# Panel order in the gates' stage, and where sums, dots and the residual stand in the merge's tail, of a two-block transformer kernel

## The reference

```python
mod_x = (silu(c) @ ada_w + ada_b).reshape(6, D)          # six rows of 1024; rows 2 to 5 are used here
x_z, x_u, x_v, x_gates = ...                             # columns of hx @ w_in
y_gdn = rms_norm(o_x, gdn_norm_g) * silu(x_z)            # o_x from the scan
u = gelu(x_u); v = layer_norm(gelu(x_v))                 # the spatial gating unit
y_sgu = u * (W_s v + b)                                  # a 128x128 mixer over positions, 8 groups
g_a, g_b = split(sigmoid(x_gates))
merged = g_a * (y_gdn @ w_a) + g_b * (y_sgu @ w_b)
x = x + mod_x[2] * (merged @ w_o)
h = rms_norm(x) * (1 + mod_x[4]) + mod_x[3]              # goes to the router and the experts
# and, for the second block, whose turn comes later:
mod_2 = silu(c_2) @ w_ada_2[0] + b_ada_2[0]              # 3 rows for x, and 3 for the context
```

## Time and profile before

| what | value |
|---|---|
| median of 3 runs | 1771.29 us (1769.92 to 1771.68) |
| profiled execution, its own time | 1775.53 us |
| its span | 1773.8 us |
| mean granted TensorE clock | 0.915 |
| PE busy | 1546.5 us (87%) |
| DVE busy | 812.2 us (46%) |
| ACT busy | 371.3 us (21%) |
| gates' stage, first to last start on PE | 468.96 to 611.84 us |
| merge's stage, first to last start on PE | 615.75 to 725.34 us |

### The profile page before, as it was taken

How to read it: one execution, slowest core, us unless ns; L and a number is a source line. 1 busy time by engine, 2 the same in 40 slices (tenths; PEclk the granted TensorE clock), 3 DMA queues, 4 the chain that set the end, 5 groups by cost and what they waited for, 6 DMA issues and landing times. The chain is left out here.

```text
span 1773.8 us, 19527 instructions
## 1 busy us (share of the span) xinstructions
PE 1546.5 (87%) x7573; PEld 901.5 (51%) x7573; DVE 812.2 (46%) x1512; ACT 371.3 (21%) x700; POOL 190.3 (11%) x280
## 2 busy tenths in 40 slices
PE   4999968789999698876789868999889899999977
PEld 2877756578644344442234323444444447656563
DVE  2344548444536558632111123356564315576553
ACT  3222245111111100110000011000450124642230
POOL 0000016500000000001000000000350001212340
PEclk9899989677899799787899988999999899999998
DMA  9331002230577677579999992524311222121120
GB/s 351 98 95 48 1 1 50 84 85 11 183 260 258 235 275 246 226 309 411 408 366 367 388 344 103 190 95 159 103 37 35 95 68 75 48 95 48 49 72 24
DMA packets 132299, 283.62 MB, mean 160 GB/s; under 512 B 28744, under 2 KB 39272, under 8 KB 126955
## 3 DMA queue, kind: packets, MB, share of 16 engines
q1 hardware_dynamic: 128608, 266.65, 42.1%
q0 software_dynamic: 3600, 15.73, 2.2%
HBM read 312.77 MB, written 4.19 MB: 179 GB/s over the span
## 5 line engine op out<-in xcount | busy, mean ns | idle before, releaser
L2707 PE MATMUL ps<-hT,ring 128*128 128x512 f32 x256 | 114.8, 606 | 3.1 <-PEq L2614 2.7
L1395 PE MATMUL ps<-ring,hTx 128*128 128x512 f32 x256 | 112.1, 594 | 1.9 <-PEq L176 1.8
L327 DVE SCALAR_TENSOR_TENSOR ada_acc<-ring,cact,ada_acc 128x512 f32<-128x512 f32 x154 | 104.1, 747 | 0.5
L631 PE MATMUL ps<-hTx,ring 128*128 128x256 f32 x384 | 91.6, 394 | 5.3 <-PEq L176 5.3
L2342 PE MATMUL ps<-hT,ring 128*128 128x512 f32 x208 | 90.4, 592 | 0.0
L631 PEld LDWEIGHTS ps<-hTx,ring 128*128 128x128 f32 x384 | 75.1, 198 | 19.8 <-issue 8.0
L2707 PEld LDWEIGHTS ps<-hT,ring 128*128 128x128 f32 x256 | 48.9, 194 | 62.9 <-issue 62.9
L1395 PEld LDWEIGHTS ps<-ring,hTx 128*128 128x128 f32 x256 | 48.3, 191 | 60.5 <-issue 60.5
L1928 PE MATMUL ps<-ring,hTx 128*32 128x512 f32 x384 | 53.8, 711 | 26.0 <-DMA ring<-in_expert_w 26.0
L722 DVE SCALAR_TENSOR_TENSOR conv<-xpad,taps,conv 128x512 f32<-128x512 f32 (+1 forms) x96 | 63.6, 663 | 3.4
L2342 PEld LDWEIGHTS ps<-hT,ring 128*128 128x128 f32 x208 | 39.5, 190 | 48.5 <-issue 48.3
(11 more groups left out here) (528 smaller groups left out, 2745.8 us busy)
## 6 DMA issues: line engine op xcount, KB each, us to landing
ring<-in_expert_w SPq DMA_DIRECT2D x24, 2048.0 KB, 15.4
far<-in_expert_w SPq DMA_DIRECT2D x24, 2048.0 KB, 18.2
ring<-in_w_in SPq DMA_DIRECT2D x16, 2048.0 KB, 11.6
ring<-in_ada_w SPq DMA_DIRECT2D x12, 2048.0 KB, 9.5
ring<-in_w_ada SPq DMA_DIRECT2D x12, 2048.0 KB, 9.3
ring<-in_w_in_c SPq DMA_DIRECT2D x10, 2048.0 KB, 7.9
ring<-in_expert_w POOLq DMA_DIRECT2D x32, 512.0 KB
far<-in_expert_w POOLq DMA_DIRECT2D x32, 512.0 KB
```

What stands on the lines that cost most here:

```text
L327: ins = dve.scalar_tensor_tensor(out=part, in0=slot[:, kt], scalar=c[:, kt:kt + 1], in1=part, op0=ALU.mult, op1=ALU.add)
L631: ins = pe.matmul(ps[:, j % BANKS, s * L:(s + 1) * L], slot[:, kt, (j % 4) * P:(j % 4 + 1) * P], (hTc, hTx)[s][:, kt], start=(kt == 0), st ...
L1395: ins = pe.matmul(ps[:, 2 + i % BANKS], hTx[:, kt, t * P:(t + 1) * P], stream.slot(n)[:, kt], start=(kt == 0), stop=(kt == KT - 1))
L2707: ins = pe.matmul(bank, slot[:, kt, j % 4 * P:(j % 4 + 1) * P], hT[:, kt], **edge)
```

## The change

It makes three edits in the stream and the gates' stage, and two in the merge's tail.

In the gates' stage the panels' order becomes uvg0, rest0, uvg1, rest1, ... uvg7, rest7, where it was uvg0, uvg1, rest0, uvg2, rest1, ... uvg7, rest6, rest7. `uvg[1]` becomes panel 18, and is issued ahead of panel 17 in the scan's last step (`issue_ahead`). The scan's two borrowed slots swap their roles, so that the one given back early is that of panel 18. `total(k)` stands behind panel k + 1, no longer behind panel k + 2. In the merge's tail each `total` stands behind the whole `w_out` panel, and `dot(5)` and `put(4)` come ahead of both halves of the residual.

```diff
+    def issue_ahead(self, sp, n):
+        sp.wait_ge(self.used[n % RING], n // RING)
+        self.load(sp, n)
+        self.ahead.add(n)            # issue() skips the wait and load of a panel in this set
...
-        for i in range(9):
-            if i < 8:
-                uvg.append(len(stream.panels))
-                add_cols(w_in, COL_Z + (2 + i) * PANEL)
-            if i:
-                rest.append(len(stream.panels))
-                add_cols(ada, (3 + i) * PANEL)
+        for i in range(8):
+            uvg.append(len(stream.panels))
+            add_cols(w_in, COL_Z + (2 + i) * PANEL)
+            rest.append(len(stream.panels))
+            add_cols(ada, (4 + i) * PANEL)
...
-                slot_a, slot_b = (... for i in (2, 1))
+                slot_a, slot_b = (... for i in (1, 2))
...
-                                    stream.issue(sp, uvg[1] + 1)
+                                    stream.issue_ahead(sp, uvg[1])
...     (and gdn_lent[0::2] and [1::2] swap places where PE frees them)
-                                if i // TT >= 2:
-                                    total(pe, i // TT - 2)
+                                if i // TT:
+                                    total(pe, i // TT - 1)
...
-                        total(pe, 6)
                         total(pe, 7)
...     (merge: PE)
-                                if t == 0:
-                                    total(pe, 3 + i)
                             stream.free(pe, n)
+                            total(pe, 3 + i)
...     (merge: DVE)
                         put(dve, 3)
+                        dot(dve, 5)
+                        put(dve, 4)
                         residual(0)
-                        put(dve, 4)
-                        dot(dve, 5)
                         residual(1)
                         put(dve, 5)
```

More of the change, by code:

```diff
@@ L131, in __init__ @@
         self.issued = 0
+        self.ahead = set()
         self.taken = 0
@@ L140, in issue @@
             n = self.issued
-            if n >= RING and self.panels[n](self.slot(n)):
-                sp.wait_ge(self.used[n % RING], n // RING)
-            self.load(sp, n)
+            if n not in self.ahead:
+                if n >= RING and self.panels[n](self.slot(n)):
+                    sp.wait_ge(self.used[n % RING], n // RING)
+                self.load(sp, n)
             self.issued += 1
+    def issue_ahead(self, sp, n):
+        sp.wait_ge(self.used[n % RING], n // RING)
+        self.load(sp, n)
+        self.ahead.add(n)
     def free(self, eng, n):
@@ L788, in build @@
                 xk6 = vdec[:, :, :, :].rearrange("p a u c -> p (a u c)").rearrange("p (u c) -> p u c", c=P // 2)
-                slot_a, slot_b = (stream.slot(z_in[0] + i).rearrange("p k n -> p (k n)") for i in (2, 1))
+                slot_a, slot_b = (stream.slot(z_in[0] + i).rearrange("p k n -> p (k n)") for i in (1, 2))
                 sc = slot_a.rearrange("p (s u c) -> p s u c", s=TT, c=P)
@@ L1232, in _ @@
                                         if gi + 3 == GRP and not more:
-                                            for n in gdn_lent[0::2]:
+                                            for n in gdn_lent[1::2]:
                                                 stream.free(pe, n)
                                 if not more:
-                                    for n in gdn_lent[1::2]:
+                                    for n in gdn_lent[0::2]:
                                         stream.free(pe, n)
```

## The result

| | before | changed |
|---|---|---|
| median of the first three runs | 1771.29 us (1769.92 to 1771.68) | 1749.76 us (1746.95 to 1753.74) |
| ratio, 95% interval | 1 | 0.9882 [0.9850, 0.9914] |
| profiled execution, its span | 1773.8 us | 1750.8 us |
| mean granted clock in it | 0.915 | 0.925 |

One execution of the kernel before, of 3725.11 us, counts as a slow one and is left out of every comparison.

A forecast was written before the change was run, and what follows sets the result against it. The prediction took PE's standstills in the two stages, and a DVE chain in the merge's tail, as the bound. Its terms summed to -15.6: from 1775.53 to 1759.9, less 4.2 for the median, 1755.7 us; range 1752.0 to 1762.5.

The forecast's parts named there:

- Step 1: Gates' stage, third panel uvg[2]: it lands at 499.7 and starts there, not at 497.77, +1.9 us.
- Step 2: Gates' stage, the other panels: each slot is free just in time, so no wait, cost 0.
- Step 3: Gates' stage, mixer and gating: mixer's lateness -0.6, wait for uu -4.8, transposes and i = 14 at full clock -1.9 us.
- Step 4: End of the gates' stage: 4.8 us from first remaining sum to the merge's first pass, where it was 12.5: -7.7.
- Step 5: Merge's first panel: the clock stays at 1.00 after shorter idle times, -2.9 us; up to the tail the merge shifts whole.
- Step 6: Merge's tail: dot(5) ends 3.1 us earlier, but put(4) and residual(0) now stand behind it, +0.4 us.
- A: Rival at the merge's start: it begins at half clock all the same, 2.9 us back, total 1758.6 us; chance 0.12.
- C: Rival in the gates' stage: dots waiting for loads hold the stream, making each of panels 3 to 7 late; chance 0.04.
- How the numbers follow: The range for the whole kernel: forecast alone 1752.5 to 1759.5 us, with rivals 1752.0 to 1762.5; faster 0.93.

The follow-up runs named there:

- fill_end: The kernel before, with twelve passes of needless matmuls in PE's 5.6 us wait for dot(7) at the gates' stage's end: 1766.03 us, ratio 0.9993.
- order_alone: The kernel before with the new panel order, early issue and swapped slots, but the old places of the sums and the old merge's tail: 1773.93 us, ratio 1.0036.
- gates_only: The changed kernel with the merge's tail put back as before, so only the gates' stage is changed: 1752.50 us, ratio 0.9909.
- fill_wout: The kernel before, with six passes of needless matmuls in PE's 3 us wait for the first w_out panel: 1769.63 us, ratio 1.0009.
- sums_alone: The kernel before with the gates' sums one panel earlier, panel order and merge's tail as before: 1758.11 us, ratio 0.9949.
- dots_old: The changed kernel with DVE's old order in the merge's tail (residual(0), put(4), dot(5)), sums still behind whole panels: 1757.94 us (2 runs).

## Why the prediction was wrong

**The two edited stages, term by term** (us, forecast against the traces). Step 1, the third panel: 1.9, measured 2.2; it landed as forecast, near 499.5, and PE's transposes ahead of it waited too (1.19 us). Step 2: no wait in panels 3 to 7, as forecast. Step 3: the mixer's and the `uu` wait gone, transposes at full clock. Step 4: 4.8 between the first of the last sums and the merge, measured 4.84. Gates' stage together: 13.1 less, measured 13.5 (133.3 for 146.8; 133.5 and 133.2 in the other traces). Step 5: 2.9, measured 2.9. Step 6: +0.4, measured +0.3. None of the rivals came about in the changed kernel; part of what A describes did in `fill_end`, and C's effect, from another cause, in `order_alone`. Two sums of small size do not add up as they stand: the parts of the 1.9 in step 3 make 2.0, and step 6 has `residual(0)` as 2.5 in the text and 2.7 in the sum.

**The step that failed is "How the numbers follow"**: its range, with "1 us for what stands behind", and "about 0.2% (3.5 us) is what a measurement of this kernel tells from no change". In its place the runs showed a spread of 11 to 15 us over single executions. The forecast of -15.6 agrees with 15.3 (medians) and 16.5 (means) over all runs. It stood on a base, 1771.29, that was itself a draw of three: 59 runs have their median at 1768.9, 2.4 lower. And it was compared with three runs of the changed kernel, whose median, 1749.8, lies 3.8 below that of all thirteen. 2.4 and 3.8 are the 6.2 us by which 21.5 exceeds 15.3. So the size of the first measured gain was luck of two draws, and so is the miss of the lower bound by 2.2 us: 1753.6, the median of all thirteen, lies inside the range. The spread itself is 11 us for the changed kernel and 15 for the one before, and the two traces of before show with what: the clock falls or stays in stages that the change does not touch, 3 us a place. A range of 10 us with 1 for that was too narrow by its own row: the profiled execution stood 4.2 above the median, which was the sign of it. Nor is the range the sum of its parts: the bounds of steps 1 and 6 with 1 us give 1751.9 to 1762.3, and not 1752.5 to 1759.5.

**One term was missing from the sum.** Step 5 ends with "Up to the tail the merge then shifts as a whole", and it did not: the first `w_out` panel ran at full clock, 3.0 us less, in all three traces of the changed kernel and in `gates_only`, and at half clock in both of before. It has the size that `fill_wout` shows, and in `fill_wout` the medians did not show it. Whether it reaches the end in the changed kernel the runs don't settle: counted from the gates' first pass the three changed traces are some 19 us ahead at the router, while the medians end 15 to 16.5 ahead. That count leaves out what comes before: the gates' first pass lies between 467.5 and 472.8 us in the fourteen traces, and on average 2.0 us later in the changed three than in the two of before. Whether that is more than a draw is not shown.

Why the clock stayed up at that panel is open. It is not the length of the wait: half clock came behind 2.97 and 3.14 us (both traces of before), full clock behind 2.69, 2.68 and 2.94 (changed), and behind 3.17 in `sums_alone` and 3.09 in `dots_old`.

## What to carry to other kernels

When an in-order program waits for a small sum, ask behind which large work the sum was put, and who waits for its accumulator: here moving it by one panel took away two waits on another engine's queue. Such a move and an order of loads belong together; each was tested alone: the sums alone gave 9 to 10 us of the gain, and the order alone made the kernel slower. And before giving a range, see how far executions of one program lie apart, and in which stages: a median of three is a draw as well, on both sides of the comparison.

## What the runs showed that I had not expected

The length of a wait did not tell whether the clock would fall behind it. Idle times of 1.83 us ended at 1.00 in the changed kernel and at 0.64, then 0.51, in `fill_end`, and 3.17 us ahead of `w_out` at full clock in `sums_alone` where 2.97 had led to 0.50 in the kernel before. And a stage with the same work on DVE, the router's, took between 27.8 and 31.6 us, at granted clocks from 0.94 down to 0.72: that alone is more than the 3.5 us with which the prediction reckoned for a whole measurement.
